# A hybrid decoder layer on one core: another order of loads, column sums and factors in the first body, and the recurrence's input turned by DMA as two f16 halves

## What is computed

```python
def hybrid_layer(x, mem, norm_g, w_in, sb_q_g, sb_k_g, conv_w, conv_b, w_rg, b_rg, w_ig, b_ig,
                 lru_lambda, xa_q_g, xa_k_g, mem_g, w_mem_kv, w_out):
    h = rmsnorm(x, norm_g)
    proj = h @ w_in
    sb_q, sb_k, sb_v, sb_gate, lru_x, lru_gate, xa_q, xa_gate = jnp.split(
        proj, [int(c) for c in np.cumsum(IN_SPLITS)[:-1]], axis=-1)
...
    sb_out = stick_breaking_attention(q, k, v).transpose(0, 2, 1, 3).reshape(B, S, SB_WIDTH)
...
    xc = causal_depthwise_conv(lru_x, conv_w, conv_b)
    lru_out = rg_lru(xc, w_rg, b_rg, w_ig, b_ig, lru_lambda)
...
    y = jnp.concatenate([sb_out * jax.nn.silu(sb_gate),
                         lru_out * jax.nn.silu(lru_gate),
                         xa_out * jax.nn.silu(xa_gate)], axis=-1)
    return x + (y @ w_out).astype(x.dtype)
```

## Time and profile before

| | us |
|---|---|
| median of three runs | 1570.18 |
| the three runs | 1567.96, 1570.18, 1570.65 |
| the profiled execution | 1568.22 |
| its span | 1566.5 |
| PE busy | 1514.1 (97%) |
| DVE busy | 1029.6 (66%) |
| ACT busy | 882.3 (56%) |
| POOL busy | 314.7 (20%) |

### The profile page before, as it was taken

One profiled execution on the slowest core, in us unless ns is written; L12 is line 12 of the kernel. 1 busy time (PEld: TensorE's weight loads), 2 busy tenths in 40 slices (PEclk: granted clock), 3 DMA queues, 4 the chain that ended last, 5 costly groups with the idle time before them and its releaser, 6 DMA issues.

```text
span 1566.5 us, 29731 instructions
## 1 busy us (share of the span) xinstructions
PE 1514.1 (97%) x10828; PEld 741.4 (47%) x10828; DVE 1029.6 (66%) x1874; ACT 882.3 (56%) x1593; POOL 314.7 (20%) x305
## 2 busy tenths in 40 slices
PE   4899899999999999999999999999999999999996
PEld 1344444444444444444444444444444444444452
DVE  5889566766666666656676666666665667666674
ACT  5887455654455664455565446566445556544661
POOL 2122112222122222111222211222211222221120
PEclk9999999999999999999999999999999999999999
DMA  9355555456455445554545545544556454555545
GB/s 367 136 168 105 132 112 118 111 125 141 117 125 123 104 118 133 125 136 105 123 104 130 141 117 119 129 102 117 136 119 142 104 117 111 127 142 120 120 90 136
DMA packets 425928, 201.63 MB, mean 129 GB/s; under 512 B 394592, under 2 KB 395040, under 8 KB 424736
## 3 DMA queue, kind: packets, MB, share of 16 engines
q1 hardware_dynamic: 425600, 200.98, 52.8%
q10 hardware_dynamic: 288, 0.13, 0.0%
HBM read 55.53 MB, written 50.53 MB: 68 GB/s over the span
## 4 chain that ended last, share of the span: by engine, by line
PE 87%; ACT 4%; DVE 4%; SPq 2%; issue 2%; DMA 1%; POOL 0%; ACTq 0%; DVEq 0%; POOLq 0%
PE bank L1792 26%; PE bank L1793 26%; PE bank L1794 26%; PE bank L1871 2%; SPq L492 2%; PE bank L1986 2%; PE bank L1836 2%; PE bank L1857 1%; PE bank L1880 1%; ACT w_pair L867 1%; PE bank L1926 0%; PE bank L1921 0%; PE bank L1823 0%; PE bank L1923 0%; PE bank L1922 0%
## 5 line engine op out<-in xcount | busy, mean ns | idle before, releaser
L1792 PE MATMUL bank<-w_pair,x_hi 128*128 128x512 f16 x1536 | 585.0, 381 | 13.8 <-DVE w_pair L1231 4.8
L1793 PE MATMUL bank<-w_pair,x_hi 128*128 128x512 f16 x1536 | 584.1, 380 | 0.0
L1794 PE MATMUL bank<-w_pair,x_lo 128*128 128x512 f16 x1536 | 584.0, 380 | 0.0
L1124 ACT ACTIVATE spare<-xy,columns 128x1024 f16<-128x1024 f32 x32 | 36.7, 1148 | 399.6 <-DVE columns L1650 399.6
L1792 PEld LDWEIGHTS bank<-w_pair,x_hi 128*128 128x128 f16 x1536 | 150.7, 98 | 190.1 <-issue 13.9
L1794 PEld LDWEIGHTS bank<-w_pair,x_lo 128*128 128x128 f16 x1536 | 150.7, 98 | 182.6 <-issue 2.4
L1793 PEld LDWEIGHTS bank<-w_pair,x_hi 128*128 128x128 f16 x1536 | 150.8, 98 | 166.4 <-issue 2.5
L1792 PE MATMUL bank<-wo_pair,y_hi 128*128 128x512 f16 x480 | 181.9, 379 | 1.2 <-issue 1.2
L1793 PE MATMUL bank<-wo_pair,y_hi 128*128 128x512 f16 x480 | 181.9, 379 | 0.0
L1794 PE MATMUL bank<-wo_pair,y_lo 128*128 128x512 f16 x480 | 181.9, 379 | 0.0
L736 POOL TENSOR_TENSOR fail_and_take<-fail_and_take,seen 128x512 f32<-128x512 f32 x32 | 42.5, 1327 | 684.2 <-ACT fail_and_take L888 684.2
(11 more groups left out here) (267 smaller groups left out, 2397.8 us busy)
## 6 DMA issues: line engine op xcount, KB each, us to landing
xy<-in_x SPq DMA_DIRECT2D x32, 512.0 KB, 3.6
spare<-in_x SPq DMA_DIRECT2D x31, 512.0 KB, 4.2
out<-spare SPq DMA_DIRECT2D x30, 512.0 KB, 2.7
gate_kept<-gate SPq DMA_DIRECT2D x32, 256.0 KB, 2.3
v_kept<-v_sb SPq DMA_DIRECT2D x32, 256.0 KB, 2.1
fail_and_take<-v_sb SPq DMA_DIRECT2D x64, 128.0 KB, 2.3
q_kept<-q_t SPq DMA_DIRECT2D x32, 256.0 KB, 4.0
k_kept<-k_t SPq DMA_DIRECT2D x32, 256.0 KB, 4.5
```

Of the source, the lines that this page charges most:

```text
L1124: act.activation(y_halves[:, 0, :], xy[:, :], ACT.Copy, scale=y_top[:, :]).then_inc(s["y_high"], 1)
L1792: pe.matmul(dst, hi[:, k, :], pair[:, 0, k, :], start=k == 0, stop=False)
L1793: pe.matmul(dst, hi[:, k, :], pair[:, 1, k, :], start=False, stop=False)
L1794: last = pe.matmul(dst, lo[:, k, :], pair[:, 0, k, :], start=False, stop=k == KD - 1)
```

## The change

It has three parts.

**Loads.** SP no longer waits for the identity ahead of chunk 0, the turned rows of tile 0 come after the two small loads, and chunks 2 and 3 come ahead of the memory and its weights.

**First bodies.** Column sums, maxima and factors of a chunk are made one step earlier than before on ACT, DVE and PE: chunk_sum(0) ahead of rows_high, chunk_factor(0) ahead of rows_low, the factor of chunk c+1 ahead of the low halves of chunk c+1 and behind those of chunk c, each chunk_wide one place earlier. Memory work moves behind.

**The LRU input.** ACT writes an f16 high half into lx_halves in place of f32 lx_raw. DVE adds one operation in silu_lru, from PSUM, for the low half. SP turns both halves in one DMA transpose (128 x 512 f16, to lx_turned) ahead of the first q turn; it waits for gate_l. PE's two transposes a tile are gone, with their waits; one of these moves to gate_products. DVE makes conv_in by adding the two turned halves in place of a copy from PSUM. The taps carry the scale that ACT's copy used to apply: one small operation once.

```diff
--- before.py
+++ after.py
...
-        lx_raw = sb("lx_raw", [P, LW])
+        lx_halves = sb("lx_halves", [P, 2, LW], F16)
...
         rs_diag = spare[:, 2 * D + LW:2 * D + LW + P]
+        lx_turned = spare[:, 2 * D + LW + P:2 * D + 2 * LW + P].bitcast(F16).rearrange("p (a h t) -> p a h t", a=2, t=P)
...
         g_in = given[:, 0:KD]
         g_mem = given[:, KD:2 * KD]
         at = 2 * KD + LH * TAPS
+        taps = given[:, 2 * KD:at]
         cw = given[:, 2 * KD:at].rearrange("p (h j) -> p h j", j=TAPS)
         cb, brg, big, lam = [given[:, at + i * LH:at + (i + 1) * LH] for i in range(4)]
         gq, gk, gxq, gxk = [given[:, at + 4 * LH + i:at + 4 * LH + i + 1] for i in range(4)]
...
         HEADS = bank[7]
 
 
-        names = """turned_lx lx_evac k_gained qk_high qk_low k_halo out0_read scores sig masked scan w w_high w_low heads
+        names = """lx_evac k_gained qk_high qk_low k_halo out0_read scores sig masked scan w w_high w_low heads
             q_read k_read xa_read lru_read sg_read v_hi v_read q_sum k_sum xq_sum rs_mid rs_done normed
             gate_x gate_l gate_sb xa_scores mx_done neg_done p_done p_high p_low
             conv gates_done gates_read tanh_done beta_steps ui_done beta_done u_done h_done
...
         w_turned = sem("w_turned")
         p_turned = sem("p_turned")
         y_turned = sem("y_turned")
+        lx_arrived = sem("lx_arrived")
         late_y_high = sem("late_y_high")
         x_loaded = sem("x_loaded")
         xt_loaded = sem("xt_loaded")
...
                 sp.dma_start(staged_out(7, slice(6, KD)), w_out_g[1][:, 6:KD, :]).then_inc(stage_loaded[3], 16)
 
             sp.dma_start(xy[:, :], x_t[0]).then_inc(x_loaded, 16)
-            sp.dma_start(x_t32[:, :, :], x_turned[0]).then_inc(xt_loaded, 16)
             sp.dma_start(given[:, :], per_partition).then_inc(const_loaded, 16)
             sp.dma_start(gate[:, 0, 0:4 * HD], gain_rows).then_inc(const_loaded, 16)
-            sp.wait_ge(ident_moved, 32)
+            sp.dma_start(x_t32[:, :, :], x_turned[0]).then_inc(xt_loaded, 16)
             load_chunk(0)
             load_chunk(1)
             have(sp, s["x_sq"], 0)
             sp.dma_start(xy[:, :], x_t[1]).then_inc(x_loaded, 16)
+            load_chunk(2)
+            load_chunk(3)
             sp.dma_start(mem_raw, mem_v).then_inc(mem_loaded, 16)
             sp.dma_start(kv_raw, w_kv_v).then_inc(kv_loaded, 16)
-            load_chunk(2)
-            load_chunk(3)
             sp.dma_start(blocks[:, :, :, :], gate_blocks).then_inc(blocks_loaded, 16)
 
 
...
                     have_dma(sp, kept["q"], n - 1)
                     have(sp, s["xa_scores"], n - 1)
                     for part, signal in ((0, s["qk_high"]), (1, s["qk_low"])):
+                        if part == (1 if last else 0):
+                            have(sp, s["gate_l"], n)
+                            have(sp, s["lx_evac"], n - 1)
+                            if isinstance(n, int) and n == 0:
+                                sp.wait_ge(m_kv, MT)
+                            turn(lx_turned.rearrange("p a h t -> p (a h) t"), lx_halves[:, :, :].rearrange("p a c -> p (a c)"), lx_arrived)
                         have(sp, signal, n)
                         q_half, k_half, xq_half = halves_of_heads(n, part)
                         turn(q_t[:, part], q_half, qk_turned)
...
                 if first:
                     chunk_high(0)
                     chunk_sum(1)
+                    chunk_sum(2)
+                    chunk_high(1)
+                    chunk_sum(3)
                     row_squares()
-                    chunk_high(1)
-                    chunk_sum(2)
                 def key_halo():
 
                     have(act, qk_turned, n - 1, 96)
...
                     act.activation(squares, PROJ[0][:, :], ACT.Square, scale=unscale[:, G_Q:G_Q + 1]
                                    ).then_inc(s["q_read"], 1)
                 if first:
-                    chunk_sum(3)
                     chunk_high(2)
-                    memory_rows()
+                    chunk_sum(4)
 
                 if early:
                     out_sum(6)
...
                     act.activation(squares, PROJ[1][:, :], ACT.Square, scale=unscale[:, G_K:G_K + 1]
                                    ).then_inc(s["k_read"], 1)
                 if first:
-                    chunk_sum(4)
                     chunk_high(3)
+                    memory_rows()
+                    chunk_sum(5)
                 if early:
                     act.wait_ge(fail_ones, 1)
                     sigmoids(1)
...
                     act.activation(gate[:, p, D - HX * HD:D], PROJ[0][:, HX * HD:GC], ACT.Sigmoid, scale=u
                                    ).then_inc(s["xa_read"], 1)
                 if first:
-                    chunk_sum(5)
                     chunk_high(4)
                 if B and not (after or early):
                     weights_high(1)
...
                 if A:
                     have(act, proj_done[3], n)
                     u = unscale[:, G_LRU:G_LRU + 1]
-                    act.activation(lx_raw[:, :], PROJ[1][:, 0:LW], ACT.Copy, scale=u)
+                    have_dma(act, lx_arrived, n - 1)
+                    act.activation(lx_halves[:, 0, :], PROJ[1][:, 0:LW], ACT.Copy, scale=VDOWN)
                     act.activation(gate[:, p, D // 2:D // 2 + LW], PROJ[1][:, LW:GC], ACT.Sigmoid, scale=u
                                    ).then_inc(s["lru_read"], 1)
 
...
                 if first:
                     heads_high()
                     memory_values(1)
+                if isinstance(n, int) and n < 0:
+                    chunk_sum(0)
                 if X and not first:
                     rows_high()
                 if isinstance(n, int) and n == 2:
...
                     if A:
                         have(act, qk_turned, n, 96)
                     act.activation(y_halves[:, 0, :], xy[:, :], ACT.Copy, scale=y_top[:, :]).then_inc(s["y_high"], 1)
-                if isinstance(n, int) and n < 0:
-                    chunk_sum(0)
 
             act.wait_ge(ident_rows_made, 2)
             act.dma_start(ident_flat, ident_rows).then_inc(ident_moved, 16)
...
                 early = isinstance(n, int) and n == 1
                 third = isinstance(n, int) and n == 2
 
-                def next_chunk(c):
-
+                def next_factor(c):
+
+                    chunk_factor(c)
                     chunk_top(c + 1)
-                    chunk_factor(c)
                     chunk_rows(c + 1)
-                    chunk_low(c)
 
                 def row_diagonal():
                     have(dve, s["x_rs"], n + 1)
...
                     dve.tensor_scalar(diagonal_of(n + 1), ident[:, :], rs_x[:, :], None, ALU.mult).then_inc(s["x_diag"], 1)
 
                 if first:
-                    chunk_factor(0)
                     chunk_low(0)
                     chunk_top(1)
                     chunk_rows(1)
-                    chunk_factor(1)
+                    next_factor(1)
                     chunk_low(1)
+                    next_factor(2)
                     row_diagonal()
                     for m in range(MT):
                         memory_turned(m)
-                    chunk_top(2)
-                    chunk_rows(2)
+                if isinstance(n, int) and n < 0:
+                    chunk_top(0)
                 last_one, after, end = near_end(n)
 
                 def convolution(d):
 
-                    have(dve, s["turned_lx"], n - d)
+                    have_dma(dve, lx_arrived, n - d)
                     dve.tensor_copy(conv_in[:, :, 0:TAPS - 1], conv_in[:, :, P:P + TAPS - 1]).then_inc(s["halo"], 1)
                     have(dve, s["halo"], n - d)
-                    dve.tensor_copy(conv_in[:, :, TAPS - 1:], SMALL[:, 2 * P:4 * P].rearrange("p (h t) -> p h t", t=P)
-                                    ).then_inc(s["lx_evac"], 1)
+                    dve.tensor_tensor(conv_in[:, :, TAPS - 1:], lx_turned[:, 0, :, :], lx_turned[:, 1, :, :], ALU.add
+                                      ).then_inc(s["lx_evac"], 1)
                     have(dve, s["lx_evac"], n - d)
                     if isinstance(n, int) and n == 1:
                         dve.wait_ge(qk_turned, 96)
...
                 if A:
                     head_sums(s["q_read"], s["q_sum"], 0, HS)
                 if first:
-                    next_chunk(2)
+                    chunk_low(2)
+                    next_factor(3)
                 if early:
                     memory_values_split()
                     memory_keys_turned()
...
                 if A:
                     head_sums(s["k_read"], s["k_sum"], HS, HS)
                 if first:
-                    next_chunk(3)
+                    chunk_low(3)
+                    next_factor(4)
                 if third:
                     chunk_low(6, 3)
                 if B and not after:
...
                     weights_low(1)
 
```

(31 more changed lines are left out.)

## The result

The changed kernel takes 1573.35 us (median of 8 runs, 1570.80 to 1574.39) against 1568.87 for the kernel before (8 runs): the ratio is 1.0026, with a 95% interval of 1.0017 to 1.0035. It is slower by 4.5 us. Run again beside the later experiments it gave 1573.08, ratio 1.0030 [1.0018, 1.0041].

The account below looks back on a forecast made before the run. PE bounds the kernel, with SP's queue a second bound 0.58 us a body away. 1568.2 - 6.7 (PE) + 11.2 (SP) + 0.4 (DVE) - 3.5 (first body) = 1569.6, plus 2.0 for the median: 1571.6 us, range 1564 to 1581.

Parts of the forecast that it names:

- the 2.0 added for the median: End of the sum: 2.0 us added because the runs' median, 1570.18, lay 2.0 above the profiled execution.
- PE's saving: Switch from projection to scores on PE: 0.21 us less a tile without the two transposes, times 32 tiles, -6.7.
- The shift on SP: SP's queue: the added turn moves the q turn and everything up to x_lo 0.93 us later a body.
- The wait at project(0): PE waits for x_lo: shift less the 0.58 margin, 0.35 us a body, +9.5 over 27 bodies.
- Bodies 3 to 5: Early-body waits behind SP's queue: +0.8 us in body 3, +0.9 in body 5; body 4 counted at the steady 0.35.
- DVE's operation ahead of the gate: The low half adds 0.4 us on DVE, felt only in body 1 where project(5) waits for the gate: +0.4.
- The first body: Start of the kernel: earlier loads and factors made a step ahead give 1.6 + 1.9, -3.5 us.
- Hidden: Rival, SP's queue: the turn holds SP so briefly that project(0) has no wait; median 1560.5 us, chance 0.13.
- Not hidden at all: Rival, SP's queue: shift of 1.25 us, wait of 0.67 a body at project(0); median 1580.8, chance 0.20.
- The first body gives nothing: Rival, kernel start: loads come earlier but memory or identity sets the same end; median 1575.1 us, chance 0.15.
- within: Whole kernel: a result between 1567.0 and 1573.3 us, not told from no change at about 0.2%; chance 0.45.

Follow-up runs that it names:

- e1: The changed kernel with the turn of the LRU input moved from ahead of the first q turn to right behind x_lo's turn on SP: 1562.72 us, ratio 0.9953.
- e3: The changed kernel with a plain DMA of the same bytes in place of the LRU input's transpose, in all bodies but the first: 1562.32 us, ratio 0.9954.
- e8: The changed kernel itself run and profiled once more, nothing changed: 1573.08 us, ratio 1.0030.
- e2: The changed kernel with its LRU input part undone, keeping only the new loads and first-body order: 1566.81 us, ratio 0.9987.
- e5: e1 with SP waiting for the identity between chunk 0 and chunk 1: 1561.69 us, ratio 0.9953.
- e7: The changed kernel with the LRU turn right ahead of x_hi's turn, behind those of q, k and the weights: 1585.07 us, ratio 1.0099.
- e4: The changed kernel turning only the high half of the LRU input (128 x 256 f16) in all bodies but the first: 1572.27 us, ratio 1.0018.

## Why the prediction was right, and where it was off

The prediction was 1571.6 in a range of 1564 to 1581; measured 1573.35. Against the kernel before it said +1.4 and it was +4.5, or +2.6 and +4.1 in the two profiles. The absolute number came nearer than the difference by luck: the 2.0 added for the median was that of three runs (1570.18), and over eight the median of the kernel before is 1568.87, 0.65 above its profile.

**PE's saving**: 0.21 a tile, from the two switches of rows 2. Measured 0.22 (46.35 to 46.13 in e1 and e3). Right, and the upper bound of 0.53 was not near.

**The shift on SP**: 0.93 from one hold and one wait. Between ACT's last high half and the q turn it is 1.02 less 0.09, 0.93. Right, and by the mechanism named: e3 and e1 take away the hold or the place, and the loss goes. The text's own terms give a little less than it states: 627.8 + 1.19 + 0.12 is 0.91 behind 628.20, the least is 0.81 and not 0.85, and the most is 1.31 and not 1.25. The queue was not quite without a gap either: around the kept gate and ahead of x_hi the kernel before has pauses of 0.2 to 0.3 in place of 0.12. They did not shrink, so they took nothing of the shift up.

**The wait at project(0)**: 0.35 a body expected. By the bodies' length it is 0.36 (46.49 - 46.13), or 0.38 in e8, all of it at the start of project(0): PE's other matmuls keep the offsets that they have in e1. The waits listed are less, 0.3 to 0.5 in every other body and none in most of those between, since the end of the last matmul covers some of it: project(0) starts 0.5 late in one and 0.2 in the other. Right in size; that it falls unevenly on the pair of bodies I had not said. Against the start of its body ACT's last high half ends at 29.45 in one and at 29.27 in the other, and x_lo's turn is 13.01 behind the q turn in the one and 12.83 in the other. The first difference is there in e1 too (29.43 and 29.26), where PE hides it; what holds the turn for the second I can't say.

**Bodies 3 to 5**: I gave body 5 0.9 and body 3 0.8. Body 3's wait for DVE's L1434 grew from 3.6 to 4.4, 0.8, and e2 (3.5) and e3 (3.8) show that it is the turn on SP that does it. From body 3 to body 6 the loss is 1.6, and 1.4 in e8, where my terms, less the 0.21 each, give 1.0.

**DVE's operation ahead of the gate**: +0.4 in body 1 expected, and 0.33 measured (a wait of 1.61 for one of 1.28). Body 2 was left at nothing, and there the same wait is 0.67, 0.76 in e8, where before it was 0.10. That is a term missed.

**The first body**: -3.5 expected, -2.2 measured in the first profile and -3.25 in the second. The difference is the pace of the first matmuls (the first 24 took 6.74 before, 7.79 and 6.61 in the two executions of the changed kernel); with that taken out it is -3.3 and -3.1. So the size was about right, but two of its steps were off, and they cancelled, which is luck. The first: I let chunk 0 land at 11.1, right behind the small loads; it landed at 12.8. Issue and landing of the turned rows of tile 0 and of chunk 0 in the changed kernel:

```profile
x_t<-in_x_turned SPq DMA_DIRECT2D x1, 512.0 KB, 5.4
```

```profile
wo_pair<-in_w_in SPq DMA_DIRECT2D x1, 2048.0 KB, 10.1
```

The turned rows, issued at 2.19, landed at 7.6, and chunk 0, issued at 2.66, at 12.8: about my own 4.9 for a chunk, counted from the load that now stands ahead of it, and not from the small ones. The steps behind it took 7.9 in place of 8.4, so the first matmul came 2.2 earlier and not 3.3. The identity, which came at 14.7, had no part in it (table under e5). The second: behind the first matmul I gave the body 0.2 more, and it gained 1.1. The first memory product went from 42.68 to 43.40 and not to 41.1, since DVE's chain ahead of it was longer than I worked out (memory_turned ended at 43.25, not 41); behind it PE's waits of 1.3 and 0.6 shrank to one of 1.1. That the first product of 8 matmuls took 3.67 in place of 5.30 is not a gain: in the kernel before the clock is 0.50 in 44 to 46, on that product, and in the changed one it is 0.50 in 34 to 36, on other work.

**What the sum misses.** In e8's execution, which had its low clock at body 1 like that of before, the parts are (expected in brackets): the first body -3.25 (-3.5), bodies 1 and 2 +1.5 (+0.8), bodies 3 to 5 +1.4 (+1.0), the 25 bodies from 6 on +4.1 (+3.5), the end +0.4 (-0.2). Every part is off to the same side, none by more than 0.7. The one with a cause shown is the wait for the gate in body 2.

**The rivals.** "Hidden" (a transpose holds SP like a plain DMA) is wrong here: e3 stands for that kernel, and it took 1562.32. The Trainium skill's sentence on it (Advanced Engine Details and Errata, section X-Bar Transpose (TRN2)), that transposes are as fast as regular DMAs, may be true of the transfer: from issue to landing the turn took 2.4 and the plain copy of e3 2.0. Of the time on the issuing queue these runs show 1.19 against 0.50 for the same bytes. "Not hidden at all" was priced by the same sum, 0.67 a body and 1580.8, and e7 is what it would have been: 0.75 and 1585.07. "The first body gives nothing" fell with e2.

**The chances.** By the bound of 0.2% the result is slower, to which I had given 0.36, less than the 0.45 of "within". The forecast stood only 1.7 under the edge, and several small errors to the same side took it over.

## What to carry to other kernels

When work is moved from the busiest engine to a queue, read not how busy that queue is but the margin between the last thing it brings and the instruction that needs it, and price the insertion by what one instruction holds the queue for, not by its bytes. If the margin is smaller than the price, look for a place in the queue behind the critical transfer: here the same turn, further down the queue, made a loss of 0.26% into a gain of 0.47% (0.13% of it from the first body). A load that starts earlier lands behind whatever stands ahead of it: count the bytes in front. And before a microsecond between two profiles is explained, compare the granted clock and the pace of equal matmuls in the same stretches: here they made up 1.1 us of body 0 and 1.7 us of body 1.

## What the runs showed of the hardware

- A DMA transpose held SP for 1.17 with 128 x 256 f16 (e4), for 1.19 with 128 x 512 and for 1.23 to 1.27 with 128 x 1024 (x_hi, x_lo): the hold hardly went with the size. A plain DMA of the 128 KB of the 128 x 512 turn held it for 0.50 (e3).
- A 64 KB DMA of another queue took 2.1 from issue to landing before any 2 MB load was issued, 7.4 beside one (e5) and 9.5 beside two.
- Behind one and the same stand of PE of 2.51 the granted clock was 0.57 and 0.58 over 4 us in two executions and 1.00 in a third (the changed kernel's first), and body 1 took 42.73, 43.18 and 41.49.
- After PE's nearly idle start matmuls of 512 columns followed each other at 0.43 and then at 0.22, 8 to 13 of them at the slow pace in executions of one program, while the granted clock read 1.00.
- So the early bodies of the same program differ between executions by up to 1 us (body 1 of the changed kernel at 82.61 and at 81.59, body 3 at 176.49 and at 177.34), and a gain of 1 us there is at the edge of what two profiles can show.
